# Sample pages for the NSA compression: both head groups in one load, turned by products with the identity

## The chip, the cores and the metric

The kernel runs on one core of a Trainium2 chip. The metric is the device time of one execution in microseconds. Every kernel is executed several times, and the median of the runs is given. The engines are named as in the profile: PE (TensorE, matrix products; PEld is its weight load), DVE (VectorE), ACT (ScalarE), POOL (GpSimd) and SP (SyncE, which here only issues transfers; SPq is its queue).

## The reference, cut to what matters

One inference step of a hybrid decoder layer: a prompt of 1024 positions and 8 samples with one new position and 512 cached positions each. The cache is paged, 128 positions to a page, 4 pages to a sample. Four head groups share the mixing: attention with a forget bias ("fox"), NSA (compressed, selected and window branch), pooling, and memory. The change touches the compression of the NSA group. For keys (kind 0) and values (kind 1) it takes the rows of each block of 64 positions and of each of the 2 head groups as one vector of 4096 numbers, adds a position term, and sends it through a small network:

```python
def nsa_compress(rows, pe, w1, w2):
    B, L, G, dh = rows.shape
    nb = L // NSA_BLOCK
    blk = rows.reshape(B, nb, NSA_BLOCK, G, dh) + pe[:, None, :].astype(rows.dtype)
    flat = jnp.transpose(blk, (0, 1, 3, 2, 4)).reshape(B, nb, G, NSA_BLOCK * dh)
    hid = jax.nn.silu(jnp.einsum('bngf,fe->bnge', flat, w1))
    return jnp.einsum('bnge,ed->bngd', hid, w2)
```

For the samples, `rows` are the pages of `cache_nsa_kv[page, position, kind, group, channel]`, with 4 kinds, 2 groups and 64 channels, so that the two groups of one kind and position lie side by side: 128 numbers, 512 bytes.

## The kernel before, in words

All five engines run one hand-written list of steps, `STEPS`, each in its own program. PE's part of a step runs in that order, and the other engines take its results in the same order. The steps that matter here:

- `project(m)` computes column tile m of the input projection for all 1032 positions: 72 products of 344 columns (three for each of 8 depths and 3 column chunks, L485 to L487), about 11.3 us at full clock. Its weights are loaded by SP (`load_w`, issue at L1879) and split into a high and a low part by POOL (L1778 and L1780).
- `natural(m)` turns a projected tile back to positions by rows, and copies it out through two banks, one copied by ACT ("A") and one by DVE ("D").
- `forget` computes running sums of the forget gates on DVE; SP then moves them (L1944), and only behind that does it issue weight tile 10.
- `pair` 0 to 7 (keys) and 8 to 15 (values) each bring the 4 pages of one sample into the layout of the compression: PE turns them into one bank (`pair_job`, L643), and ACT (even pairs) or DVE (odd pairs, L1483) copies the bank, 128 x 512, to FT. An even pair uses bank A and an odd one bank D; a job waits until the bank's last result has been copied.
- `compress(kind)` multiplies FT by the first weight matrix, which SP loads in four pieces of 1 MB (L1907) into two slots; a slot is loaded again when PE has read it. PE's products are at L661: 16 for each piece, shown as 32 records.
- `attend(0)`, `(1)`, `(2)` are the attention over the prompt: memory, fox, and selected with window.

SP issues all loads in one list. A quarter q is half a sample's pages of one kind, that is two pages: `load_pair(q)`. Quarters 0 to 3 are issued before weight tile 9, then 4 to 6, 7 to 9, 10 to 12 and 13 to 15 behind weight tiles 10, 11, 12 and 13, 16 to 19 before the fox attention, 20 to 22 with the first two compression weight pieces, 23 and 24 between the third and the fourth piece, 25 to 27 behind the fourth, and 28 to 31 when pairs 8 and 9 have been turned. A page's number is read from the page table (L1883) and then its transfers are issued (L1900): one for each head group, 64 partitions of two runs of 256 bytes. A partition j of a page's half holds positions 2j and 2j + 1 of the page (r = 0, 1).

PE turns a quarter's page pair with the transpose instruction, once for each group: the result has (r, channel) on its 128 partitions and (page, j) on its columns.

Order of PE's steps in the first stretch: project 8, forget, pair 0, project 9, pairs 1 and 2, project 10, natural 9, project 11, pair 3, natural 10, pair 4, project 12, natural 11, pair 5, natural 12, pairs 6 and 7, attend 1. In the second: project 13 and 14, natural 13, compress 0, project 15, pairs 8 to 11, project 16, natural 15, pairs 12 to 15, compress 1.

Of the kernel before, what the change touches and what calls it, by code (L numbers as in the profile page):

```python
# [29 lines left out]
P = 128  # L30
# [7 lines left out]
DH = 64  # L38
# [114 lines left out]
def build(nc, x_p, x_s, c_fox, c_lf, c_nsa, st_win, st_pool, c_mem, ptab, mem_p, norm_g, w_in, b_f, pe_, w1,  # L153
# [3 lines left out]
    with ExitStack() as ctx:  # L157
        def sb(name, shape, dt=F32):
            return ctx.enter_context(nc.sbuf_tensor(name, shape, dt))

        def sem(name):
            return ctx.enter_context(nc.semaphore(name))
# [16 lines left out]
        ident = sb("ident", [P, P])  # L179
# [75 lines left out]
        def pair_slot(q):  # L255


            if q < 16:
                where = PP[:, q * 256:(q + 1) * 256]
            elif 20 <= q < 28:  # L260
                where = NAT[:, (q - 20) * 512 + 256:(q - 19) * 512]
            else:
                where = VW[:, q % 4 * 256:(q % 4 + 1) * 256]
            return where.rearrange("p (a c) -> p a c", a=2)

        w1s = PP[:, :].rearrange("p (s j e) -> p s j e", s=2, j=8)
        HS = KW[:, 0:2 * R_ALL].rearrange("p (a r) -> p a r", a=2)
# [92 lines left out]
        s_pair = [sem(f"s_pair{n}") for n in range(NB)]  # L360
# [84 lines left out]
        def _(pe):  # L445
            mm, tr = nc.tensor.matmul, nc.tensor.transpose
            nA, nD = [0], [0]

            def job_a():

                if nA[0]:
                    pe.wait_ge(s_fA, nA[0])
                nA[0] += 1
                return bk(6)

            def job_d():

                if nD[0]:
                    pe.wait_ge(s_fD, nD[0])
                nD[0] += 1  # L460
                return bk(7)
# [174 lines left out]
            def pair_job(n, kind):  # L636

                out = job_a() if n % 2 == 0 else job_d()
                pe.wait_ge(s_pair[n], 128 * (kind + 1))
                for a in range(2):  # L640
                    q = 16 * kind + 2 * n + a
                    for g in range(2):
                        last = tr(out[:, (2 * g + a) * P:(2 * g + a + 1) * P],  # L643
                                  pair_slot(q)[:, g, :], ident[:, :])
                last.then_inc(s_TA if n % 2 == 0 else s_TD, 1)
                mark["pair", kind, n] = (s_TA, nA[0]) if n % 2 == 0 else (s_TD, nD[0])

# [268 lines left out]
            for step, n in STEPS:  # L916
# [10 lines left out]
                elif step == "natural":  # L927
                    if n == 18:
                        pe.wait_ge(s_fD, mark["cmp_scores", 0][1])
                    natural(n)  # L930
                elif step == "pair":
                    pair_job(n % 8, n // 8)
                elif step == "attend":
                    if n == 0:
# [920 lines left out]
        def _(sp):  # L1855
# [25 lines left out]
            def page(i):  # L1881

                return sp.value_load(ptb[0:1, bass.ds(i, 1)], min_val=0, max_val=c_fox.shape[1] - 1)  # L1883

            def load_pair(q):

                kind, n, half = q // 16, (q % 16) // 2, q % 2
                if q == 0:
                    sp.wait_ge(s_on, PHASE[0][1])
                if q == 20:  # L1890
                    sp.wait_ge(s_nst, 32)
                if q >= 28:
                    sem_, val = mark["pair", 1, (q - 28) // 2]
                    sp.wait_ge(sem_, val)
                for a in range(2):
                    pg = page(NPG * n + 2 * half + a)
                    for g in range(2):
                        src = c_nsa[0, bass.ds(pg, 1), :, kind, g, :].rearrange("o (j r) d -> (o j) r d", r=2)
                        dst = pair_slot(q)[a * DH:(a + 1) * DH, g, :].rearrange("p (r d) -> p r d", r=2)
                        sp.dma_start(dst, src).then_inc(s_pair[n], 16)  # L1900

            def load_w1(n):
                kind, c = n // 4, n % 4
# [31 lines left out]
            for q in range(4):  # L1935
                load_pair(q)
# [9 lines left out]
            for n in range(5):  # L1946
                load_w(10 + n)
                if n < 4:
                    for q in range(4 + 3 * n, 7 + 3 * n):
                        load_pair(q)  # L1950
# [4 lines left out]
            for q in range(16, 20):  # L1955
                load_pair(q)
# [36 lines left out]
            for g, w in enumerate(POOLW):  # L1993
                src = st_pool[0, :, 16 - w:15, g * DH:(g + 1) * DH]
# [62 lines left out]
            for m in (28, 29, 30):  # L2057
                load_w(m)
                n = m - 28
# [106 lines left out]
```

## Time and profile before

| | |
|---|---|
| median of 3 runs | 949.19 us (948.94 to 949.86) |
| profiled execution | 949.2 us, span 947.5 us |
| PE busy | 826.5 us (87%), 5755 products |
| DVE / ACT / POOL busy | 385.0 / 268.7 / 164.0 us |
| DMA | 79.45 MB in 110409 packets, 27237 of them under 512 B |
| granted clock of PE, mean | 0.946 of full speed |

The span is the time from the first to the last instruction of the profiled execution; 1.7 us of its time lie around it. Busy time is not the same as time that matters: an engine that waits for another costs nothing unless it is on the chain that ended last. That chain is the view to begin with. A line such as `L643` is a line of the kernel's source; `out<-in` gives the program's names of what is written and read. The bracket at the end of a timeline's row gives the idle time of the engine before it, and what ended it. The clock is given as a share: 1.00 is 2.4 GHz, 0.50 is 1.2 GHz.

### The profile page before, as it was taken

To read this page: it belongs to the slowest core of one execution; us is meant where nothing else is said; L and a number is where in the kernel's file an instruction comes from. 1 tells how busy PE (TensorE), PEld (TensorE's weight loads), DVE (VectorE), ACT (ScalarE), POOL (GpSimd) and SP (SyncE) were. 2 spreads that over 40 slices of the span, in tenths; PEclk is the share of its full clock that TensorE was granted. 3 is DMA by queue.
4 is the path that set the end of the run, shared out by engine and by line. 5 is a ranking of instruction groups with operands and counts; after the bars stand their busy time and mean duration, and the time that the engine had idled before them with its cause. 6 is when DMAs were issued, how large, how long until landed. Compare 5 with 4: busy or idle time off the path is not lost.

```text
span 947.5 us, 15437 instructions
## 1 busy us (share of the span) xinstructions
PE 826.5 (87%) x5755; PEld 680.9 (72%) x5755; DVE 385.0 (41%) x752; ACT 268.7 (28%) x624; POOL 164.0 (17%) x115
## 2 busy tenths in 40 slices
PE   3788997896999879895987999989999999699997
PEld 3788687893566878795964666659888878567775
DVE  3721734113664201201335767773823115434433
ACT  4612710112544202200124444540113225221211
POOL 4645001331000301046211000001431110000000
PEclk9979998996999989997899999989999999879999
DMA  7410002235411234131031000001124547256531
GB/s 231 160 48 23 1 21 50 55 75 171 150 45 49 81 106 128 24 105 45 1 114 42 2 1 2 1 4 47 46 82 143 149 135 201 84 188 193 180 121 48
DMA packets 110409, 79.45 MB, mean 84 GB/s; under 512 B 27237, under 2 KB 104308, under 8 KB 110264
## 3 DMA queue, kind: packets, MB, share of 16 engines
q1 hardware_dynamic: 108880, 77.66, 27.4%
q10 hardware_dynamic: 1456, 0.82, 0.4%
q8 instruction: 46, 0.75, 0.3%
q14 instruction: 27, 0.22, 0.1%
HBM read 68.81 MB, written 13.85 MB: 87 GB/s over the span
## 4 chain that ended last, share of the span: by engine, by line
PE 71%; DVE 9%; SPq 5%; issue 4%; DMA 4%; POOL 3%; ACT 3%; DVEq 0%; POOLq 0%; ACTq 0%
PE PS L485 14%; PE PS L487 13%; PE PS L486 13%; PE PS L567 6%; PE PS L613 5%; PE PS L592 4%; PE PS L661 3%; SPq L1900 2%; PE PS L577 2%; PE PS L871 2%; DVE AUG L1390 1%; PE PS L787 1%; PE PS L617 1%; DVE stat L1340 1%; SPq L2022 1%
## 5 line engine op out<-in xcount | busy, mean ns | idle before, releaser
L485 PE MATMUL PS<-HH,WH 128*128 128x344 f32 (+2 forms) x824 | 285.9, 347 | 21.7 <-POOL WL L1780 13.8
L486 PE MATMUL PS<-HL,WH 128*128 128x344 f32 (+2 forms) x824 | 280.5, 340 | 0.0
L487 PE MATMUL PS<-HH,WL 128*128 128x344 f32 (+2 forms) x824 | 280.0, 340 | 0.0
L485 PEld LDWEIGHTS PS<-HH,WH 128*128 128x128 f32 x824 | 162.0, 197 | 35.1 <-POOL WL L1780 14.4
L486 PEld LDWEIGHTS PS<-HL,WH 128*128 128x128 f32 x824 | 161.7, 196 | 6.4
L487 PEld LDWEIGHTS PS<-HH,WL 128*128 128x128 f32 x824 | 161.4, 196 | 6.8
L1778 POOL TENSOR_TENSOR WH<-WR,onesc 128x1024 fp32r<-128x1024 f32 x31 | 60.4, 1949 | 560.8 <-issue 224.9
L1105 ACT ACTIVATE PP<-PS,stat 128x640 f32<-128x640 f32 (+7 forms) x96 | 67.8, 710 | 106.9 <-DVE stat L1340 106.9
L1340 DVE TENSOR_REDUCE stat<-PS 128x1 f32<-128x640 f32 (+7 forms) x96 | 65.1, 720 | 65.1 <-PE PS L580 64.7
L1780 POOL TENSOR_TENSOR WL<-WR,WH 128x1024 fp32r<-128x1024 f32 x31 | 79.0, 2548 | 2.4
L592 PE MATMUL PS<-ident,PP 128*128 128x128 f32 x472 | 66.3, 277 | 10.7 <-DVE AUG L1390 8.2
L567 PE MATMUL PS<-AUG 64*128 64x512 f32 (+3 forms) x288 | 61.8, 536 | 9.8 <-ACT PP L1105 7.4
L592 PEld LDWEIGHTS PS<-ident,PP 128*128 128x128 f32 x472 | 53.7, 141 | 16.6 <-DVE AUG L1390 14.0
L1390 DVE COPY AUG<-PS 128x512 f32<-128x512 f32 (+3 forms) x80 | 48.9, 627 | 8.3 <-PE PS L592 7.7
L613 PE MATMUL PS<-AUG,NAT 128*64 128x128 f32 (+1 forms) x640 | 47.4, 290 | 4.0 <-ACT AUG L997 1.9
L661 PE MATMUL PS<-OB,PP 128*128 128x161 f32 x256 | 41.5, 328 | 9.7 <-DMA PP<-in_nsa_w 5.2
L1311 DVE COPY VS<-PS 64x8 f32<-64x8 f32 x8 | 1.4, 170 | 118.2 <-PE PS L487 118.2
L661 PEld LDWEIGHTS PS<-OB,PP 128*128 128x128 f32 x256 | 40.2, 211 | 10.8 <-DMA PP<-in_nsa_w 6.0
L567 PEld LDWEIGHTS PS<-AUG 64*128 64x128 f32 x288 | 25.2, 195 | 30.4 <-issue 19.3
L613 PEld LDWEIGHTS PS<-AUG,NAT 128*64 128x64 f32 x640 | 35.5, 137 | 11.4 <-DVE AUG L1390 4.1
L997 ACT ACTIVATE AUG<-PS 128x128 f32<-128x128 f32 (+5 forms) x88 | 40.9, 465 | 7.5 <-PE PS L592 7.0
L1638 DVE COPY NAT<-PS 128x512 f32<-128x512 f32 x16 | 11.1, 692 | 62.9 <-PE PS L787 62.7
(318 smaller groups left out, 862.9 us busy)
## 6 DMA issues: line engine op xcount, KB each, us to landing
WR<-in_w_in SPq DMA_DIRECT2D x26, 512.0 KB, 4.3
PP<-in_nsa_w SPq DMA_DIRECT2D x8, 1024.0 KB, 6.1
OB<-in_x_prompt SPq DMA_DIRECT2D x8, 512.0 KB, 5.8
out<-NAT SPq DMA_DIRECT2D x2, 2048.0 KB, 7.7
PP<-in_cache_fox_kv SPq DMA_DIRECT2D x32, 128.0 KB, 2.3
PP<-in_cache_nsa_kv SPq DMA_DIRECT2D x64, 64.0 KB, 1.9
PP<-in_state_nsa_win SPq DMA_DIRECT2D x16, 256.0 KB, 3.0
PP<-in_cache_mem_kv SPq DMA_DIRECT2D x16, 256.0 KB, 3.3
```

The source lines that it names most:

```text
L485: mm(out, lhs[0], rhs[0], start=(k == 0), stop=False)
L486: mm(out, lhs[0], rhs[1], start=False, stop=False)
L487: return mm(out, lhs[1], rhs[0], start=False, stop=(k == KC - 1))
L567: mm(bk(score_bank(u, e) + c // 4)[:, 0:n * P], q[r, i * P:(i + 1) * P], k[r, (k0 + c) * P:(k0 + c + n) * P], start=True, stop=False)
L592: last = tr(bk(4 + g % 3)[:, (b - c) * P:(b - c + 1) * P], PP[:, p0:p0 + P], ident[:, :])
L613: mm(bk(7)[e * DH:(e + 1) * DH, 0:wide * P], v, p_, start=(b == 0), stop=(b == (1 if what == "mem" else nk - 1)))
L661: last = mm(bk(e)[:, 0:R_ALL + 1], w1s[:, n % 2, jj, e * P:(e + 1) * P], FT[:, j, :], start=(j == 0), stop=(j == NJ - 1))
L1105: last = act1(PP[:, c:c + nk * P], flat(score_bank(u, e), nk), ACT.Exp, bias=stat[:, k:k + 1], accum_out=stat[:, 16 + k:17 + k])
L1340: v.tensor_reduce(stat[:, k:k + 1], flat(score_bank(u, e), nk), AX.X, ALU.max, negate=True).then_inc(s_nm, 1)
L1390: v.tensor_copy(turned_p(u - 1, e, c, n), bk(4 + g % 3)[:, 0:n * P]).then_inc(s_cD, 1)
L1778: g.tensor_tensor(hi_, WR[:, s, :, :], ones, ALU.mult).then_inc(s_wcp, 1)
L1780: g.tensor_tensor(lo_, WR[:, s, :, :], hi_.bitcast(F32), ALU.subtract).then_inc(s_split, 1)
```

## The change

A page's keys or values of one kind come in one transfer with both head groups (two runs of 512 bytes for each of 64 partitions) instead of two transfers (two runs of 256 bytes each). 64 transfers are issued instead of 128, and the semaphore counts are halved to match. In the buffer, a partition now holds (r, group, channel) where it held (group, r, channel). The turn of one group therefore reads 64 columns for r = 0 and 64 for r = 1, which are no longer adjacent: each is a plain product with the identity as the moving operand, which writes 64 partitions of the bank. A pair job has 8 products where it had 4 transpose instructions. Bank, copies and everything after them are unchanged.

```diff
-            return where.rearrange("p (a c) -> p a c", a=2)
+            return where.rearrange("p (r c) -> p r c", r=2)
...
-                pe.wait_ge(s_pair[n], 128 * (kind + 1))
+                pe.wait_ge(s_pair[n], 64 * (kind + 1))
                 for a in range(2):
                     q = 16 * kind + 2 * n + a
                     for g in range(2):
-                        last = tr(out[:, (2 * g + a) * P:(2 * g + a + 1) * P],
-                                  pair_slot(q)[:, g, :], ident[:, :])
+                        for r in range(2):
+                            last = mm(out[r * DH:(r + 1) * DH, (2 * g + a) * P:(2 * g + a + 1) * P],
+                                      pair_slot(q)[:, r, g * DH:(g + 1) * DH], ident[:, :], start=True, stop=True)
...
                     pg = page(NPG * n + 2 * half + a)
-                    for g in range(2):
-                        src = c_nsa[0, bass.ds(pg, 1), :, kind, g, :].rearrange("o (j r) d -> (o j) r d", r=2)
-                        dst = pair_slot(q)[a * DH:(a + 1) * DH, g, :].rearrange("p (r d) -> p r d", r=2)
-                        sp.dma_start(dst, src).then_inc(s_pair[n], 16)
+                    src = c_nsa[0, bass.ds(pg, 1), :, kind, :, :].rearrange("o (j r) g d -> (o j) r (g d)", r=2)
+                    sp.dma_start(pair_slot(q)[a * DH:(a + 1) * DH], src).then_inc(s_pair[n], 16)
```

## Rows read from the trace of the kernel before

**Rows 1.** Page, section 4: shares of the ending chain by line.
```profile
PE PS L485 14%; PE PS L487 13%; PE PS L486 13%; PE PS L567 6%; PE PS L613 5%; PE PS L592 4%; PE PS L661 3%; SPq L1900 2%; PE PS L577 2%; PE PS L871 2%; DVE AUG L1390 1%; PE PS L787 1%; PE PS L617 1%; DVE stat L1340 1%; SPq L2022 1%
```

**Rows 2.** Lines L1900 and L2022: issue in ns, min/median/max, first and last start.
```profile
L1900 SPq DMA_DIRECT2D PP<-in_cache_nsa_kv x64: 537/537/1108, 125.3 to 214.1; - x64
...
L2022 SPq DMA_DIRECT2D PP<-in_cache_nsa_kv x64: 332/333/1544, 696.8 to 907.4; - x64
```

**Rows 3.** Chain of waits in two stretches: start us, us, what.
```profile
170.80 2.01 DMA PP<-in_cache_nsa_kv
...
343.17 0.55 SPq L1900
343.90 0.54 SPq L1900
```

**Rows 4.** Chain: four turns, eight turns, eight products (16 records).
```profile
201.82 0.44 PE PS L643 x4
...
219.52 1.91 PE PS L643 x8
...
284.69 1.02 PE PS L613 x16
```

**Rows 5.** Timeline of SP's queue: start us, us, line, what.
```profile
125.30 16.64 SPq L1900 DMA_DIRECT2D PP<-in_cache_nsa_kv  x16
...
143.19 0.40 SPq L1879 DMA_DIRECT2D WR<-in_w_in  x1
...
162.45 0.42 SPq L1879 DMA_DIRECT2D WR<-in_w_in  x1
163.86 11.50 SPq L1900 DMA_DIRECT2D PP<-in_cache_nsa_kv  x12
...
348.56 0.59 SPq L1907 DMA_DIRECT2D PP<-in_nsa_w  x1
```

**Rows 6.** Timeline of POOL, splits of tiles 9 and 10 [idle before].
```profile
149.88 1.89 POOL L1778 TENSOR_TENSOR WH<-WR,onesc 128x1024 fp32r<-128x1024 f32 x1 [54.82 <-DMA WR<-in_w_in]
...
169.21 2.35 POOL L1780 TENSOR_TENSOR WL<-WR,WH 128x1024 fp32r<-128x1024 f32 x1
```

**Rows 7.** Timeline of PE, projection 9 and pair 2 [idle before].
```profile
154.25 0.65 PE L485 MATMUL PS<-HH,WH 128*128 128x344 f32 x1 [2.55 <-POOL WL L1780]
...
172.94 0.78 PE L643 MATMUL PS<-ident,PP 128*128 128x128 f32 x4 [4.24 <-DMA PP<-in_cache_nsa_kv]
```

**Rows 8.** Stretches: PE, PEld, DVE, ACT, POOL busy; granted clock; DMA.
```profile
154.30:159.50 5.20, 5.20 (x18) 5.20 (x19) 4.91 (x6) 0.00 (x0) 0.00 (x0) 0.50 0.00 0
173.50:176.50 3.00, 3.00 (x13) 3.00 (x12) 0.00 (x0) 1.11 (x1) 0.00 (x0) 0.50 0.17 38
219.30:221.50 2.20, 2.12 (x10) 1.38 (x8) 0.74 (x2) 1.09 (x1) 2.12 (x2) 0.50 0.11 42
388.00:391.60 3.60, 2.45 (x16) 1.65 (x16) 1.58 (x2) 2.18 (x3) 0.00 (x0) 1.00 0.12 27
```

**Rows 9.** Timeline of PE, compression pieces and pairs 8 to 15.
```profile
346.29 6.32 PE L661 MATMUL PS<-OB,PP 128*128 128x161 f32 x32 [2.16 <-DMA PP<-in_nsa_w]
354.36 4.66 PE L661 MATMUL PS<-OB,PP 128*128 128x161 f32 x32 [1.75 <-DMA PP<-in_nsa_w]
...
372.03 1.09 PE L643 MATMUL PS<-ident,VW 128*128 128x128 f32 x8 [1.06 <-ACT KCs L997]
...
387.98 1.23 PE L643 MATMUL PS<-ident,NAT 128*128 128x128 f32 x8 [0.79 <-ACT NAT L997]
...
391.02 0.63 PE L643 MATMUL PS<-ident,VW 128*128 128x128 f32 x4 [0.55 <-DMA VW<-in_cache_nsa_kv]
```

**Rows 10.** Timeline of DVE, copy of pair 15.
```profile
391.68 1.07 DVE L1483 COPY OB<-PS 128x512 f32<-128x512 f32 x1 [1.35 <-PE PS L643]
```

**Rows 11.** Timeline of PE, first scores of two attention phases.
```profile
222.88 3.78 PE L567 MATMUL PS<-AUG 64*128 64x512 f32 x8 [1.47 <-DVE OB L1483]
...
494.21 1.99 PE L567 MATMUL PS<-AUG 64*128 64x512 f32 x8 [0.98 <-DVE VW L1328]
```

## The prediction

> **What bounds the kernel now.** I read the page's chain first, then the chain piece by piece, then the queue of SP, POOL and PE over the two stretches in which sample pages are turned (124 to 223 us and 303 to 394 us). The chain is TensorE for the most part: the three products of every projection are 40% of it, and the issuing of the page loads (SP at L1900) holds 2% [rows 1]. That 2% is what the change can take away, and TensorE is where it pays. A load is issued in 537 ns [rows 2] and lands 2.0 us later; two successive issues of one page start 0.73 us apart [rows 3], so each load that goes takes 0.73 us out of SP's queue. There are 128 loads, 4 per quarter q; 64 go.
>
> Where does SP's queue end a wait? Three places. (a) Project 9: weight tile 9 is issued at 143.19, behind the first 16 page loads (125.30 to 141.94) [rows 5]; POOL splits it from 149.88 [rows 6], and PE, done with pair 0 at 154.25 - 2.55 = 151.7, waits 2.55 us for POOL before project 9 [rows 7]. (b) Project 10: pair 2, which stands before it on PE, waits 4.24 us for pages [rows 7] that are issued only after weight tile 10 at 162.45 [rows 5]. (c) Compression of the keys: its fourth weight piece is issued at 348.56 behind eight page loads [rows 5], and PE waits 1.75 us for it [rows 9]. Elsewhere the pages are ahead of PE, save 0.55 us before pair 15 [rows 9].
>
> **What the change removes: SP's issues.** Per quarter it takes 2 of 4 loads, 1.46 us. I keep 537 ns and 2.0 us for the new load, which has as many pieces, each twice as long. The bounds for its issue are 0.33 us, what L2022 takes for a page of 64 KB, and 1.1 us, the longest at L1900 [rows 2]. The lower one would bring no more than 0.4 us, since in (a) to (c) something else is late next.
>
> (a) The first four quarters end 8 x 0.73 = 5.8 us earlier, so tile 9 is issued at 137.4 and split by about 148.4 (154.2 - 5.8). Then pair 0 is late next, and project 9 starts straight behind it, at about 152.2. Today it runs at half clock to 159.5 [rows 8]; without the gap I expect full clock. What project 9 gains so is idle time again: tile 10 cannot leave before 162.45, because its issue waits for the forget sums, which the change does not touch, and POOL ends its split at 169.21 + 2.35 = 171.56 [rows 6].
> (b) Pair 2 needs four pages after 163.86. Three issues fewer stand before the last (one for each page before it, and the last page has a single load): 170.80 [rows 3] - 4 x 0.73 = 167.9, landed at 169.9 instead of 172.8. With its 1 to 2 us (below) it ends at 170.9 to 171.9, and the split ends at 171.56: project 10 starts at about 171.8 instead of 173.72. That is **-1.9 us**, its new cost on pair 2 included. Project 10 runs its first 3 us at half clock today [rows 8]; as pair 2 stands in part of that stretch, I take another **-0.5** (0 to -1.3).
> (c) The fourth piece leaves 4 x 0.73 = 2.9 us earlier, at 345.6, and lands at 351.4. Late next is PE's own third piece, which ends at 346.29 + 6.32 = 352.6. So the fourth starts 1.8 us earlier, not 2.9: **-1.8 us**. The third piece's weight load shares the DMA engines with half as many page packets; I give that nothing (0 to -0.4).
> The 16 loads of the last four quarters get 5.8 us shorter too, but win only the 0.55 us before pair 15, which the next part swallows. Loads at 227 and 305 us run beside attention and projections 13 and 14; cover is many us, so they are worth nothing. The waits on pair semaphores (64 instead of 128 counts for half the loads) stay where they are.
>
> **What it adds: TensorE.** A pair job is now 4 turns of 128 x 128: 0.44 us at full clock, 1.91/2 = 0.96 us at half [rows 4]. It becomes 8 products with 64 columns of pages held and 128 columns of identity moving, in plain f32. That form is in the trace: the weighing of values at L613 (held 128 x 64, moving 128 x 128, two halves of the output in turn) takes 1.02 us for 8 products, shown as 16 records [rows 4]. That is 0.58 more than 0.44; a part of it is the start of the first one, which today's job has too, so I take **1.0 us, +0.5 for each job**, and at half clock 2.0, +1.0. The rest of a job, one copy of 128 x 512 (1.07 us, [rows 10]), keeps its shape. Which of the 16 jobs lie on the path?
> Pairs 0, 1: hidden in the idle time of (a). Pair 2: counted in (b). Pair 3: hidden by VectorE, which first takes project 11. Pair 4 stands directly before project 12: +0.5. Pair 5 is at full clock, its copy gates the rest of natural 12: +0.5. Pairs 6 and 7 run back to back at half clock, 1.91 us [rows 4, 8], before attention: +2.0. Together **+3.0**.
> Pairs 8 and 9 stand back to back (372.03, 1.09 us), then 10 and 11 wait for their copies [rows 9]; the second of each couple follows VectorE's copy of the one before. The series 8, 9, copy, 11 grows by 3 x 0.5: +1.5 on the start of project 16. After natural 15 the series is 12, 13, copy, 15: pair 13 starts behind pair 12 and a copy of natural 15 that end together, so 0.4 to 0.5 of pair 12's growth shows, 13 and 15 add 1.0, and the 0.55 us wait for pages before pair 15 [rows 9] is gone: +0.9. Together **+2.4**.
>
> **Sum**: -1.9 - 0.5 - 1.8 + 3.0 + 2.4 = +1.2 us. The profiled execution took 949.2 us (span 947.5), the median of the runs is 949.19, so no correction between them: **950.4 us**. Own range 948.0 to 951.8. This kernel's measurement can tell about 0.2%, 1.9 us, from no change.
>
> **Rivals.**
> *The clock comes back earlier.* The change puts plain products where turns were. At 219.3 to 221.5 PE is busy 2.12 of 2.20 us with turns alone, and the clock stays at its lower level of 1.2 GHz [rows 8]; the first unit of the forgetting attention then starts at that level and takes 3.78 us for its scores, where the like unit of the later attention, at 2.4 GHz, takes 1.99 [rows 11]. If the products hold or raise the clock there, pairs 6 and 7 cost 2.0 instead of 4.0 us and the first scores gain 1.8: 950.4 - 2.0 - 1.8 = **946.6 us**. For it: those rows. Against it: from 388.0 to 391.6 us PE does nothing but turns, with gaps, and the clock stays full [rows 8], so turns do seem to hold it. The Trainium skill (TensorE: Matmul & The Clock Gate, Part 4: PE-mode transpose) says that turns don't count as busy for the clock in the way of products; by that rule this rival would be the likeliest. The trace agrees at 220 us and disagrees at 388 to 391.6 us. Chance 0.22.
> *The clock falls at pairs 12 to 15* (ends slower). They stand between gaps of 0.55 to 0.79 us today, at full clock [rows 8, 9]. If the level there is the lower one, jobs 12, 13 and 15 take 2.0 instead of 1.0 us: 950.4 + 3.0 = **953.4 us**. It decides if the level falls before pair 13, near 390 us; later it costs under 1 us. For it: the same pattern of turns, copies and gaps between 214 us and pair 6 does lose the clock, by 219.3 [rows 8]. Chance 0.18.
> *The halves don't run side by side.* Then a job takes 8 x 0.24 = 1.9 us, +0.96 more for each of some 11 growths on the path (6 counted up to attention, with the two at half clock double and pair 2; 5 after): +11, **961 us**. Against it stands L613's 1.02 us; for it, that all eight products here move the same identity. Chance 0.07.
> *The loads don't get cheaper*: twice the bytes cost SP twice, 1.1 us. Then (a), (b) and (c) fall, pair 2 adds 0.5, and 949.2 + 3.0 + 2.4 + 0.5 = **955.1 us**. Against it: weight loads of 512 KB are issued in 0.4 to 0.6 us (0.42 at 162.45) [rows 5]. Chance 0.05.
>
> **How the numbers follow.** Forecast 0.48, rivals 0.22, 0.18, 0.07 and 0.05. The range goes from just below the first rival to the second, 946.2 to 953.5: the last two rivals (0.12) and tails (0.08) are outside. Faster by over 0.2% (below 947.3): the first rival and a rest of the forecast, less the first rival's upper part: 0.24. Slower (over 951.1): second to fourth rivals less a part of the second, and the forecast's upper end: 0.30. Within 0.2%: 0.46.
>
> **What would show it.** SP: page periods 0.73 us shorter, tile 9 issued near 137.4, the fourth compression piece near 345.6. PE: project 9 right behind pair 0 at full clock; project 10 near 171.8; the fourth piece directly behind the third, no wait for weights. A pair job of 16 records in 1.0 us at full clock. First scores of the forgetting attention at 223.5 (222.88 - 1.9 - 0.5 + 3.0), and [rows 9] pair 15 behind pair 13's copy. The forecast is wrong if the granted clock differs from today's in 214 to 231 or in 386 to 399 us, or if a job's length isn't 1.0 us.

## The result, and the profile after

The changed kernel took 945.21 us (median of 9 runs, 942.46 to 946.32), the kernel before, run between them, 949.86 (9 runs, 947.97 to 953.75). The ratio is 0.994, with a 95% interval of 0.9921 to 0.996: faster by 0.6%. The forecast was 950.4 in a range of 946.2 to 953.5, so it had the sign wrong and the time fell 1 us below the range. The profiled execution took 943.73 us, its span 942.0 (before 949.2 and 947.5).

Page of the changed kernel: span, and the chain's shares by engine and by line. Its line numbers are one higher than before's in the body, and one lower from L1899 (the page loads, L1900 before) on.
```profile
span 942.0 us, 15629 instructions
...
PE 74%; DVE 9%; issue 4%; POOL 4%; DMA 3%; ACT 3%; SPq 2%; DVEq 0%; POOLq 0%; ACTq 0%
PE PS L485 15%; PE PS L487 14%; PE PS L486 14%; PE PS L567 6%; PE PS L613 5%; PE PS L592 4%; PE PS L662 3%; PE PS L788 2%; PE PS L872 2%; PE PS L577 2%; DVE AUG L1391 1%; DVE stat L1341 1%; PE PS L617 1%; DMA PP<-in_nsa_w 1%; POOL OB L1843 1%
```
The page loads, 2% of the chain before [rows 1], are no longer among the lines that it names. The chain itself, in order of time, still runs over them, ahead of pair 2 and of the fourth compression piece (start us, us, what):
```profile
165.70 0.54 SPq L1899
166.99 2.31 DMA PP<-in_cache_nsa_kv
169.44 1.09 PE PS L644 x16
...
339.65 0.54 SPq L1899
340.23 6.74 DMA PP<-in_nsa_w
```

SP's queue: the lines view of L1899 (issue in ns, min/median/max), then its timeline (start us, us).
```profile
L1899 SPq DMA_DIRECT2D PP<-in_cache_nsa_kv x32: 537/537/719, 125.3 to 195.3; - x32
```
```profile
125.32 9.82 SPq L1899 DMA_DIRECT2D PP<-in_cache_nsa_kv  x8
...
136.79 0.84 SPq L1880 DMA_DIRECT2D WR<-in_w_in  x1
158.47 2.98 SPq L1943 DMA_DIRECT2D KW<-AUG  x4
161.50 0.42 SPq L1880 DMA_DIRECT2D WR<-in_w_in  x1
162.93 7.19 SPq L1899 DMA_DIRECT2D PP<-in_cache_nsa_kv  x6
...
340.23 0.59 SPq L1906 DMA_DIRECT2D PP<-in_nsa_w  x1
```
A load of twice the bytes is issued in the same 537 ns as before [rows 2], and half of them go. Four quarters take 9.8 us, not 16.6 [rows 5], so here each issue that goes saves 0.85 us. Weight tile 9 leaves at 136.8 and the fourth compression piece at 340.2. Tile 10 leaves at 161.5, 0.95 us earlier than before, though the forecast had nothing move it.

TensorE's timeline (start us, us, [idle before]); L644 is a pair job, 16 records each.
```profile
147.78 0.60 PE L707 MATMUL PS<-ident,lf 128*4 128x128 f32 x4
...
151.63 1.98 PE L644 MATMUL PS<-ident,PP 128*64 128x128 f32 x16
153.54 0.61 PE L485 MATMUL PS<-HH,WH 128*128 128x344 f32 x1
...
169.44 1.09 PE L644 MATMUL PS<-ident,PP 128*64 128x128 f32 x16 [3.08 <-DMA PP<-in_cache_nsa_kv]
...
181.90 0.27 PE L536 MATMUL PS<-ident,AUG 128*128 128x128 f32 x1
...
215.81 1.97 PE L644 MATMUL PS<-ident,PP 128*64 128x128 f32 x32
219.15 1.99 PE L567 MATMUL PS<-AUG 64*128 64x512 f32 x8 [1.36 <-DVE OB L1484]
```
```profile
340.26 4.65 PE L662 MATMUL PS<-OB,PP 128*128 128x161 f32 x32 [1.78 <-DMA PP<-in_nsa_w]
347.01 4.66 PE L662 MATMUL PS<-OB,PP 128*128 128x161 f32 x32 [2.10 <-DMA PP<-in_nsa_w]
...
364.68 1.97 PE L644 MATMUL PS<-ident,VW 128*64 128x128 f32 x32 [1.06 <-ACT KCs L998]
...
384.43 1.97 PE L644 MATMUL PS<-ident,VW 128*64 128x128 f32 x32 [0.32 <-ACT OB L998]
```
Two pair jobs take 1.97 us, at 215.81 as at 364.68. At 215.81 that is what two jobs of turns took before at half clock (1.91, [rows 4]), because here the clock is full. The first scores take 1.99 instead of 3.78 us [rows 11].

Windows of the changed kernel (columns as [rows 8]).
```profile
154.30:159.50 5.20, 5.20 (x35) 5.20 (x34) 4.01 (x5) 0.49 (x1) 0.00 (x0) 1.00 0.01 3
170.60:173.60 3.00, 3.00 (x20) 3.00 (x21) 0.00 (x0) 1.11 (x1) 0.00 (x0) 1.00 0.76 207
213.00:218.00 5.00, 4.19 (x56) 3.37 (x56) 1.94 (x3) 1.64 (x2) 1.46 (x1) 1.00 0.08 29
```
The third number from the right is the granted clock. All three of these stretches, the starts of projections 9 and 10 and the jobs before attention, run at the upper level, 2.4 GHz, where before they ran at 1.2 GHz [rows 8].

**Stages.** I cut each trace at rows of TensorE: t0, the first turn of the forget sums (147.78 above); n9 and n11, the first instruction of natural jobs 9 and 11 (181.90 and 209.80); att, the first scores of the forgetting attention (219.15); 3rd, the scores of its third unit; p13, projection 13; c1 and c2, the first instructions of the two compressions (327.59 and 388.97); p8, pair 8 (364.68). Two traces of a kernel stand as a/b; the experiments are told below.

| us | before | after | loads only | products only | tile 9 first | turns in 5-7 | after, new order | before, new order | hybrid |
|---|---|---|---|---|---|---|---|---|---|
| start to t0 | 147.8/145.7 | 147.8/148.8 | 149.7/149.6 | 147.3/147.3 | 145.7 | 149.4/145.3 | 147.8 | 145.6 | 147.7 |
| t0 to n9 | 38.6/38.5 | 34.1/33.8 | 34.8/34.7 | 39.4/39.1 | 38.6 | 35.2/36.0 | 29.3 | 27.3 | 30.8 |
| n9 to n11 | 27.1/27.1 | 27.9/27.9 | 27.2/27.2 | 27.9/27.9 | 27.1 | 27.9/27.9 | 27.9 | 32.9 | 27.9 |
| n11 to att | 9.5/9.4 | 9.4/9.3 | 9.4/9.4 | 10.3/9.4 | 9.3 | 8.4/9.3 | 9.4 | 9.0 | 9.4 |
| att to 3rd | 17.0/15.9 | 14.8/15.1 | 16.9/16.9 | 14.8/14.8 | 14.6 | 15.9/15.3 | 14.8 | 15.9 | 14.8 |
| 3rd to p13 | 63.2/64.9 | 63.2/64.3 | 63.2/63.2 | 63.2/63.2 | 63.2 | 64.3/63.2 | 63.2 | 64.4 | 63.2 |
| p13 to c1 | 30.4/30.4 | 30.5/30.2 | 30.4/30.4 | 28.9/28.9 | 30.4 | 30.2/28.9 | 30.5 | 30.2 | 30.4 |
| c1 to p8 | 38.6/39.0 | 37.1/36.6 | 36.3/36.4 | 41.7/41.8 | 39.0 | 36.1/37.9 | 35.0 | 36.4 | 34.3 |
| p8 to c2 | 22.2/23.4 | 24.3/24.3 | 22.0/22.0 | 24.3/24.3 | 23.4 | 24.3/24.3 | 24.3 | 23.0 | 22.4 |
| c2 to end | 553.3/551.9 | 553.0/553.3 | 552.6/552.8 | 553.9/553.8 | 551.8 | 553.8/551.2 | 552.2 | 554.3 | 554.1 |

The first row varies by 4 us between traces of one kernel (149.4 and 145.3), so nothing in it counts as an effect. Other rows vary too: "after" and "turns in 5-7" have the same code up to pair 5, and from t0 to n9 they took 34.1, 33.8, 35.2 and 36.0 us. A difference below about 1 us in a single trace, and below about 2 us in that row, is not an effect yet. By the means of two traces each, the change gained 4.5 us from t0 to n9, 1.5 from att to 3rd and 2.0 from c1 to p8; it lost 0.8 from n9 to n11 and 1.5 from p8 to c2. With the two traces of "turns in 5-7" the gain from t0 to n9 is 3.7.

### The profile page after: what moved, and what is told of

It is laid out like the page before. It is cut to its first block, busy times and chain, and to the rows that moved or that the text cites. A ratio compares the mean times of both kernels' runs of the same rounds, so it can differ in the third digit from the quotient of the medians.

```text
span 942.0 us, 15629 instructions
## 1 busy us (share of the span) xinstructions
PE 828.0 (88%) x5947; PEld 683.2 (73%) x5947; DVE 384.4 (41%) x752; ACT 269.1 (29%) x624; POOL 164.0 (17%) x115
## 3 DMA queue, kind: packets, MB, share of 16 engines
q1 hardware_dynamic: 99664, 77.65, 27.2%
## 4 chain that ended last, share of the span: by engine, by line
PE 74%; DVE 9%; issue 4%; POOL 4%; DMA 3%; ACT 3%; SPq 2%; DVEq 0%; POOLq 0%; ACTq 0%
PE PS L485 15%; PE PS L487 14%; PE PS L486 14%; PE PS L567 6%; PE PS L613 5%; PE PS L592 4%; PE PS L662 3%; PE PS L788 2%; PE PS L872 2%; PE PS L577 2%; DVE AUG L1391 1%; DVE stat L1341 1%; PE PS L617 1%; DMA PP<-in_nsa_w 1%; POOL OB L1843 1%
## 5 line engine op out<-in xcount | busy, mean ns | idle before, releaser
L1779 POOL TENSOR_TENSOR WH<-WR,onesc 128x1024 fp32r<-128x1024 f32 x31 | 61.3, 1976 | 551.9 <-issue 222.6
L592 PEld LDWEIGHTS PS<-ident,PP 128*128 128x128 f32 x472 | 53.6, 141 | 16.6 <-DVE AUG L1391 14.0
L1750 DVE TENSOR_TENSOR PP<-PS,WR 128x1024 f32<-128x1024 f32 (+1 forms) x9 | 11.0, 1223 | 62.1 <-PE PS L487 42.1
```

What stands on the lines that cost most here:

```text
L592: last = tr(bk(4 + g % 3)[:, (b - c) * P:(b - c + 1) * P], PP[:, p0:p0 + P], ident[:, :])
L1779: g.tensor_tensor(hi_, WR[:, s, :, :], ones, ALU.mult).then_inc(s_wcp, 1)
```

## The experiments

Three questions were open. Is the gain the loads' or the products'? Was it tile 9 or the pages that held the first stretch? And did products hold the clock before attention?

**The changed kernel again**, no edit.

> The changed kernel again, beside the kernel before on the same chip, as the measure for the runs of this call. Both theories expect 4 to 6 us less than before (ratio 0.994 to 0.996), tile 9 split by about 147, project 10 at about 170.5 and the first scores of the fox attention in 2.0 us.

Measured: 944.53 us (6 runs) beside 950.30 of the kernel before (25 runs), ratio 0.9928 (0.9901 to 0.9955). The next three experiments have the same comparison. The gain repeats, and the trace is the second one of "after" in the table.

**Loads alone.** The changed kernel's loads, with turns; an operand then is a page's row half of both head groups, so the turned pages land in other places and the compressions work on exchanged rows. Every instruction keeps its shape.
```diff
-                    for g in range(2):
-                        for r in range(2):
-                            last = mm(out[r * DH:(r + 1) * DH, (2 * g + a) * P:(2 * g + a + 1) * P],
-                                      pair_slot(q)[:, r, g * DH:(g + 1) * DH], ident[:, :], start=True, stop=True)
+                    for r in range(2):
+                        last = tr(out[:, (2 * r + a) * P:(2 * r + a + 1) * P],
+                                  pair_slot(q)[:, r, :], ident[:, :])
```

> The loads of the change with the turns of before: one transfer for each page, and four transpose instructions over the 128 adjacent columns for each job. The turned groups and rows come out in swapped places, so the compression of the samples computes on exchanged data; the work is the same in kind and number. Theory Q (all gain comes from SP's shorter queue; the products only cost, 0.5 us for each job on the path, some 5 of them before and after attention): about 942.5 against 949.5 of before, 2 to 3 us below the changed kernel, and the fox attention's first scores at full clock, 2.0 us. Theory P (plain products in the place of transposes keep the clock up before the attention): pairs 6 and 7 at half clock, first scores 3.8 us, no faster than the changed kernel, 945 to 947.

Measured: 943.97 us (8 runs), ratio 0.9935 (0.9904 to 0.9965). TensorE's timeline, then a window:
```profile
170.97 1.09 PE L643 MATMUL PS<-ident,PP 128*128 128x128 f32 x4 [5.59 <-DMA PP<-in_cache_nsa_kv]
...
217.49 2.11 PE L643 MATMUL PS<-ident,PP 128*128 128x128 f32 x8
220.96 3.78 PE L567 MATMUL PS<-AUG 64*128 64x512 f32 x8 [1.35 <-DVE OB L1483]
```
```profile
172.00:175.00 3.00, 3.00 (x13) 3.00 (x12) 0.00 (x0) 1.11 (x1) 0.00 (x0) 0.56 0.73 197
```
The time lies between the two theories, and each is half right: the gain is there without the products, as theory Q says, and the clock is at half at pairs 6 and 7 and in the first scores (3.78 us), as theory P says.

**Products alone.** The kernel before, with its four loads per quarter.
```diff
-                        last = tr(out[:, (2 * g + a) * P:(2 * g + a + 1) * P],
-                                  pair_slot(q)[:, g, :], ident[:, :])
+                        for r in range(2):
+                            last = mm(out[r * DH:(r + 1) * DH, (2 * g + a) * P:(2 * g + a + 1) * P],
+                                      pair_slot(q)[:, g, r * DH:(r + 1) * DH], ident[:, :], start=True, stop=True)
```

> The products of the change with the loads of before: two transfers for each page in the old layout, eight products with the identity for each job. Theory Q: project 9 still waits for POOL until about 154.2, pair 2 for pages until 172.9, the clock is lost before pairs 6 and 7, and each job on the path costs more: +3 to +6 us over before, about 954. Theory P: pairs 6 and 7 and the first scores of the fox attention run at full clock: -2 to +1 us, about 949.

Measured: 951.86 us (12 runs), ratio 1.0008 (0.9989 to 1.0028): no difference that shows, and between the 949 and 954 of the two theories. TensorE's timeline, the fourth compression piece:
```profile
354.15 6.32 PE L662 MATMUL PS<-OB,PP 128*128 128x161 f32 x32 [4.28 <-DMA PP<-in_nsa_w]
```
c1 comes 1.5 us earlier here, but the piece's load does not, so PE waits 4.28 us for it and then works at half clock: c1 to p8 is 3.0 us longer. One more trace of each half followed, at 944.12 us for the loads and 952.17 for the products, beside 947.97 of the kernel before.

> The loads of the change with turns in all jobs once more (turned groups and rows come out in swapped places). Theory P: half clock at pairs 6 and 7 and 9.3 to 9.5 us from natural 11 to the first scores. Theory R: full clock in about half of such looks, 8.4 us. The end of project 8 to natural 11 should be 61.9 us again.

> The products of the change with the loads of before once more. Theory P: pairs 6 and 7 at full clock, 2.0 us, natural 11 to first scores 9.3 to 10.3 us. Theory R: half clock in about half of such looks, then pairs 6 and 7 take 3.8 to 4.0 us and that length is 11 us or more. The end of project 8 to natural 11 should be 67.3 us again.

So the gain is the loads', and the products come out near zero over the whole kernel. The table shows why. Beside "loads only", the changed kernel pays 0.8 us from n9 to n11 (pair 4), 0.5 from c1 to p8 and 2.3 from p8 to c2. It gets back 1.9 from att to 3rd, where its clock is full and that of "loads only" half, and 0.8 from t0 to n9, where the clock at the start of projection 10 differs (0.56 in the window above, against 1.00 in [170.60:173.60] of after). The 0.8 can't be put down to the products, since the same code varies by 2.2 us there. The sum is +0.9 us, and the medians differ by 0.6, which their intervals don't separate.

**Tile 9 ahead of the pages**, in the kernel before. This gives tile 9 its early issue without taking a single page issue away.
```diff
+            load_w(9)
...
-            load_w(9)
```
The added line stands right behind `load_w(8)`, ahead of quarters 0 to 3; the removed one stood behind them.

> The kernel before with one move in SP's list: the load of weight tile 9 is issued ahead of the first 16 page loads instead of behind them. Both theories: POOL has split tile 9 before 148, VectorE's first pass over the forget sums (4 x 1024) takes 0.7 us instead of 2.07 because POOL no longer works beside it, tile 10 leaves SP 1 to 1.4 us earlier, and project 9 starts behind pair 0. Theory Q: pair 2 still waits for its pages, until about 171.8, so project 10 gains 1 us only: 948 to 948.5. If the collision of POOL and VectorE is not the cause of the 2.07 us, that pass stays at 2.07 and project 10 stays at 173.7: no change.

Measured: 950.51 us (12 runs), ratio 1.000 (0.9979 to 1.0022). Timelines of VectorE and TensorE, and a window:
```profile
151.07 0.68 DVE L1526 TENSOR_SCALAR OB<-OB 4x1024 f32<-4x1024 f32 x1
```
```profile
169.97 1.09 PE L643 MATMUL PS<-ident,PP 128*128 128x128 f32 x4 [7.11 <-DMA PP<-in_cache_nsa_kv]
```
```profile
171.00:174.00 3.00, 3.00 (x12) 3.00 (x11) 0.00 (x0) 1.10 (x1) 0.00 (x0) 0.50 0.22 49
```
Projection 9 is early, and most of that becomes idle time before pair 2: 7.11 us instead of 4.24 [rows 7]. VectorE's pass takes 0.68 us, as expected, so tile 10 and the pages behind it leave earlier. Counted from t0, pair 2 starts 0.9 us earlier than in the kernel before (24.2 us behind t0 instead of 25.2 and 25.1) and projection 10 0.6 us earlier, but projection 10 then stays longer at half clock, and t0 to n9 stays 38.6. The 948 to 948.5 us that were expected did not come; the interval, 2 us to each side, could hide a gain of that size. The early tile alone does not bring the gain of the change. The trace is that of the fastest of the 12 executions (944.76 us).

**Turns in the three jobs before attention.** The changed kernel with turns in pairs 5, 6 and 7 of the keys; with the new loads their rows come out exchanged.
```diff
+                        if kind == 0 and n >= 5:
+                            last = tr(out[:, (2 * g + a) * P:(2 * g + a + 1) * P],
+                                      pair_slot(q)[:, g, :], ident[:, :])
+                            continue
                         for r in range(2):
```

> The changed kernel with pairs 5, 6 and 7 turned by transpose instructions as before (over the 128 adjacent columns, so that for these three samples' keys groups and rows come out exchanged; the work is the same in kind as before). All that stands ahead of pair 5 is the changed kernel's. Theory P (plain products keep the clock up in this stretch, turns don't): the clock falls before pairs 6 and 7, they take 1.9 to 2.1 us although their work is half, and the fox attention starts no earlier than in the changed kernel (natural 11 to first scores 9.3 to 9.4 us). Theory R (the clock at this place depends on when the stretch falls in the run, not on the kind of instruction): full clock as in the changed kernel, pairs 6 and 7 in 0.9 us, natural 11 to first scores about 8.0 us, and 1.4 us less in all, about 943.

Measured: 945.25 us (9 runs), ratio 0.9945 (0.9922 to 0.9968). TensorE's timeline:
```profile
218.02 0.60 PE L644 MATMUL PS<-ident,PP 128*128 128x128 f32 x4
218.96 0.66 PE L644 MATMUL PS<-ident,PP 128*128 128x128 f32 x4 [0.35 <-DVE NAT L1333]
220.97 1.99 PE L567 MATMUL PS<-AUG 64*128 64x512 f32 x8 [1.35 <-DVE OB L1488]
```
Turns stand before attention, and the clock is full all the same: a job takes 0.6 us and the first scores 1.99. From natural 11 to the first scores it is 8.4 us, 0.9 less than in the changed kernel. The 943 us of theory R did not come: the whole is no faster than the changed kernel. The kernel before took 950.99 us (14 runs) in this comparison, which holds for the experiments below too. A second trace of it was taken, and one of the kernel before beside it.

> The changed kernel with turns for pairs 5 to 7 once more (for these the turned data come out exchanged). Theory P: half clock at pairs 6 and 7 this time, 1.9 to 2.1 us, natural 11 to first scores 9.3 to 9.5 us. Theory R: full clock again or not, as chance has it; with full clock 8.4 us.

> The kernel before once more, for one more look at its clock. Theory P (products keep the clock before the fox attention, turns mostly lose it): half clock at pairs 6 and 7, 1.9 to 2.1 us. Theory R (chance of the moment, independent of the kind of instruction): full clock in about half of such looks, 0.9 us. The length from the end of project 8 to natural 11 should be 65.7 us again, since it is set by waits.

Measured: 941.07 us for the turns in pairs 5 to 7 and 947.92 for the kernel before (beside 947.97 of the same kernel). The kernel before had half clock at pairs 6 and 7 again, though its first scores took 1.99 us this time. Windows of the second trace with turns in pairs 5 to 7:
```profile
214.60:215.60 1.00, 0.96 (x5) 0.97 (x6) 0.00 (x0) 0.36 (x1) 0.00 (x0) 0.50 0.00 0
215.60:218.00 2.40, 1.36 (x9) 0.88 (x7) 1.46 (x2) 1.64 (x2) 0.00 (x0) 0.95 0.22 84
```
Here the clock was at half from about 212.3 to 215.8 us, and then came back while TensorE did nothing but turns. The count over all traces: with turns in every job the clock was half at pairs 6 and 7 in six of six (before twice, "loads only" twice, tile 9 first, before in the new order in part); with products in every job it was full in six of six (one fell to half at 218.4 and was back by 221.7); with products up to pair 4 and turns behind, full in two of two (in the second from 0.3 us into pair 6 on). Counted by whether the clock fell at all between natural 11 and the first scores, it is six of six with turns in every job, one of six with products, one of two with both. How long it stayed down varies within a kernel: the two traces of the kernel before took 3.78 and 1.99 us for the first scores. The natural jobs in between are turns in every kernel. So the kind of the three jobs right before attention does not decide it. Whether the products of pairs 0 to 4 do, or the moment at which this stretch is reached, stays open.

**A new order of issues.** If the number and place of SP's issues are what binds, order should bring more than the change. Tile 9 goes ahead of all pages; tile 10 and quarters 4 to 9 go ahead of the wait for the forget sums; the last compression piece (`load_w1(3)`) goes straight behind the third. First on the changed kernel:
```diff
+            load_w(9)
...
-            load_w(9)
+            load_w(10)
+            for q in range(4, 10):
+                load_pair(q)
...
-            for n in range(5):
-                load_w(10 + n)
-                if n < 4:
-                    for q in range(4 + 3 * n, 7 + 3 * n):
-                        load_pair(q)
+            load_w(11)
+            for q in range(10, 13):
+                load_pair(q)
+            load_w(12)
+            for q in range(13, 16):
+                load_pair(q)
+            load_w(13)
+            load_w(14)
...
+            load_w1(3)
...
-            load_w1(3)
```

> The changed kernel with SP's list put in another order: weight tiles 9 and 10 and the pages of quarters 4 to 9 are issued before SP waits for the forget sums, quarters 10 to 15 behind tiles 11 and 12, and the compression's fourth weight piece ahead of quarters 23 and 24. Expected: no wait of PE for pages before pair 2, project 10 starts at about 17.5 + 2.1 = 19.6 us behind the end of project 8 instead of 22.7, fourth piece behind the third without a wait: -3 and -2 us, about 940 against 944.5 of the changed kernel. If PE's projections are held by POOL's splits instead, -2 us only.

Measured: 938.26 us (5 runs), ratio 0.9871 (0.9843 to 0.9899). TensorE's timeline:
```profile
163.77 1.97 PE L644 MATMUL PS<-ident,PP 128*64 128x128 f32 x32
...
340.06 4.65 PE L662 MATMUL PS<-OB,PP 128*128 128x161 f32 x32 [0.25 <-DMA PP<-in_nsa_w]
```
That is 1.7 us better than expected. Pairs 1 and 2 run back to back without a wait for pages, and the fourth compression piece waits 0.25 us instead of 2.10. The same edit on the kernel before:

> The kernel before with the same new order of SP's list. It tells whether the cheaper loads matter once the pages don't stand in the way of weights. Theory Q (the change pays through SP's queue alone): this order gives the kernel before more than the change did, -6 us or more to 943, and the changed kernel with this order is then no better than this one, or worse by what its products cost (up to 2 to 3 us). If the loads must be fewer in any order: tile 11 comes late behind the pages (24 loads take until about 167), project 11 waits, and this kernel stays at 947 or above.

Measured: 940.89 us (5 runs), ratio 0.9899 (0.987 to 0.9927). Timelines of SP and TensorE:
```profile
142.43 23.83 SPq L1900 DMA_DIRECT2D PP<-in_cache_nsa_kv  x24
...
169.38 0.42 SPq L1879 DMA_DIRECT2D WR<-in_w_in  x1
```
```profile
177.90 0.42 PE L485 MATMUL PS<-HH,WH 128*128 128x344 f32 x1 [3.96 <-POOL WL L1780]
```
The order alone brings about 10 us, twice what the change brought. Both expectations were half right: it gains more than the change did, and tile 11 is late. Six quarters are 24 issues and 23.8 us here, so tile 11 leaves at 169.4, eight us later than in the reordered changed kernel (161.1), and projection 11 waits 3.96 us for its split: n9 to n11 grows to 32.9. That is where fewer issues still pay under the better order. The change adds 2.6 us by the medians, but the ranges (934.20 to 938.87, 937.57 to 942.32) overlap; the stages from t0 to n11 give it 3.0 in one trace of each.

**A hybrid.** The reordered changed kernel, with the values (pairs 8 to 15) loaded by two transfers per page and turned by turns as before. There issues are hidden and TensorE is not.
```diff
-                pe.wait_ge(s_pair[n], 64 * (kind + 1))
+                pe.wait_ge(s_pair[n], (64, 192)[kind])
...
+                        if kind:
+                            last = tr(out[:, (2 * g + a) * P:(2 * g + a + 1) * P],
+                                      pair_slot(q)[:, g, :], ident[:, :])
+                            continue
...
+                    if kind:
+                        for g in range(2):
+                            src = c_nsa[0, bass.ds(pg, 1), :, kind, g, :].rearrange("o (j r) d -> (o j) r d", r=2)
+                            dst = pair_slot(q)[a * DH:(a + 1) * DH, g, :].rearrange("p (r d) -> p r d", r=2)
+                            sp.dma_start(dst, src).then_inc(s_pair[n], 16)
+                        continue
```

> The reordered changed kernel with the values (pairs 8 to 15) loaded and turned as before, two transfers for each page and transpose instructions, and the keys (pairs 0 to 7) as in the change. The products of pairs 8 to 15 cost 2.1 us on the path (24.3 against 22.2 us from pair 8 to the second compression), and the doubled loads there were worth 0.55 us: so 1.5 to 2 us less than the reordered changed kernel, about 938.5. If the clock falls at pairs 12 to 15 with turns, no gain.

Measured: 935.96 us (4 runs, 934.13 to 936.82), ratio 0.9849 (0.9821 to 0.9877): the lowest median of all, 1.5% below the kernel before. TensorE's timeline:
```profile
376.20 0.66 PE L644 MATMUL PS<-ident,VW 128*128 128x128 f32 x4 [0.60 <-ACT OB L1002]
377.61 0.63 PE L644 MATMUL PS<-ident,VW 128*128 128x128 f32 x4 [0.75 <-DMA VW<-in_cache_nsa_kv]
```
p8 to c2 falls from 24.3 to 22.4 us, though 0.75 us of waiting for pages is back before pair 15. The median is 2.3 us below that of the reordered changed kernel, but their ranges overlap, and the two profiled spans are 934.9 (hybrid) and 934.2. The hybrid's trace gains 1.9 us in this stage and loses 1.5 from t0 to n9 and 1.9 behind c2, where the two kernels run the same code. So the stage shows the gain, and the whole time does not yet.

## Why the prediction was wrong

It forecast +1.2 us; by the means of two traces the spans differ by -4.0 (942.85 against 946.85), by the medians -4.7. The miss is 5.2 us. Three terms make 7.1 of it: 2.1 from t0 to n9, 4.1 from n11 to 3rd, 0.9 from p8 to c2. The rest, +1.9, is for the most part in stretches that the change doesn't touch (+1.6 before t0, +0.6 behind c2), and so is the scatter between traces.

**What was right.** The mechanism on SP: 537 ns for the new load, 0.68 to 0.85 us for each issue that goes where I took 0.73, tile 9 at 136.8 (137.4 forecast). Project 9 ran at full clock, if 1.3 us later than forecast (153.54), since pair 0 itself was at half clock (1.98 us); as forecast, nothing hangs on that. (c): the fourth compression piece was to gain 1.8 us and c1 to p8 fell by 2.0 (1.5 between the first two traces). That the size fits is luck in part. Late next was the landing, not the third piece as I wrote, since that ran at full clock (4.65 us, not 6.32 [rows 9]); the piece landed 6.7 us after its issue, where I had counted 5.8, and the wait, which I had expected to vanish, grew from 1.75 to 2.10. A job of products takes 1.09 us alone and two take 1.97, against 0.60 for a job of turns: +0.5, as I took. Pair 4's +0.5 was measured as +0.8. From p8 to c2 I forecast +2.4: it is +2.3 between "loads only" and the changed kernel, +1.9 between the two reordered kernels that differ there, and +1.5 against the kernel before by its two traces. One of those, at 23.4, had its clock lowered at pair 11 (two jobs in 1.53 us, not 1.10). The rivals "halves don't run side by side" and "the loads don't get cheaper" are refuted by 1.97 us for two jobs and by 537 ns. (The 11 growths of the first leave one out: pair 2, pairs 4 and 5, and pairs 6 and 7 doubled are 7, and 5 come behind attention. That makes 962 us, not 961.) "The clock falls at pairs 12 to 15" is refuted too: those jobs took 1.97 us for two in every trace with products.

**Step (b), the first stretch: forecast -2.4, measured -4.5 (-3.7 with the two traces that share the code up to pair 5).** The failed part is the bound behind pair 2, that tile 10's split ends at 171.56 because "its issue waits for the forget sums, which the change does not touch". The change does touch them. Timelines of the kernel before, VectorE and POOL:
```profile
152.67 2.07 DVE L1526 TENSOR_SCALAR OB<-OB 4x1024 f32<-4x1024 f32 x1
```
```profile
151.85 2.34 POOL L1780 TENSOR_TENSOR WL<-WR,WH 128x1024 fp32r<-128x1024 f32 x1
```
And of the changed kernel:
```profile
153.12 0.68 DVE L1527 TENSOR_SCALAR OB<-OB 4x1024 f32<-4x1024 f32 x1
```
```profile
142.55 1.89 POOL L1779 TENSOR_TENSOR WH<-WR,onesc 128x1024 fp32r<-128x1024 f32 x1 [47.46 <-DMA WR<-in_w_in]
...
167.54 2.34 POOL L1781 TENSOR_TENSOR WL<-WR,WH 128x1024 fp32r<-128x1024 f32 x1
```
Before, VectorE's pass over the forget sums ran beside POOL's second split pass of tile 9 and took 2.07 us. With tile 9 early, POOL is long done and the pass takes 0.68. The forget sums, the transfers behind them, tile 10 and the pages behind it come 0.95 us earlier. The pass stood on the chain of the kernel before, so it could be read beforehand that its length counts (start us, us, what):
```profile
152.67 2.08 DVE OB L1526
```
The split then ends at 169.88 (167.54 + 2.34), 1.7 us before my bound, and no longer holds anything: pair 2 ends last, and projection 10 starts right behind it, near 170.5 where I had 171.8. That pair 2 began at 169.44 (169.9 forecast) hides two errors that partly cancel: its pages left SP 0.9 us earlier than I took, and the last landed in 2.31 us, not 2.0. The other 0.7 us of the split is tile 10's own loading: from issue to the first split pass 4.07 us against 4.79. It is 5.1 in the second trace of the kernel before and 3.9 to 4.2 in every other trace with this order, three of them with the old page loads, so I have no cause for it.

The second failed part is projection 10's clock: I took -0.5 for its half-clock start, with -1.3 as the bound, and it ran at full clock from its start in both traces of the changed kernel. That is not a sure property of the change. Projection 10's first 3 us in the two traces with turns in pairs 5 to 7, whose code is the changed kernel's up to there (one row from each):
```profile
172.25:175.25 3.00, 3.00 (x15) 3.00 (x14) 0.00 (x0) 1.11 (x1) 0.00 (x0) 0.64 0.77 217
168.54:171.54 3.00, 3.00 (x12) 3.00 (x11) 0.00 (x0) 1.11 (x1) 0.00 (x0) 0.51 0.84 210
```
From projection 10's start to n9 it is 11.4 us in both traces of the changed kernel, 12.4 and 12.8 in these two, and 12.9 in both of the kernel before. So part of the measured gain is a state of the clock that comes and goes, and what decides it stays open. "Loads only" (0.56) lies within the same spread. "Tile 9 first" shows that the end of the collision is not enough by itself: there the pages are still late, and what it brings is lost to the clock.

**Pairs 5 to 7: forecast +2.5, measured -0.1; and att to 3rd, forecast 0, measured -1.5.** This is the rival "the clock comes back earlier", at 946.6 us and a chance of 0.22. The failed step is the half clock that I took for pairs 6 and 7 and left standing for the first scores. Both traces of after show the full clock: 1.97 us for two jobs and 1.99 for the first scores. The rival's price (2.0 + 1.8) was about right: 4.1 by the two stages. In these is pair 5's +0.5, of which 0.1 shows (pair 6 starts 6.0 us behind n11, not 5.9), since natural 12 behind pair 5 was at half clock before. The gain from att to 3rd is the less certain part: "tile 9 first", with the old loads and turns, has 14.6 us there too. Taken with the extra 2.1 of (b) the rival gives 950.4 - 3.8 - 2.1 = 944.5, close to the two medians (945.2 and 944.5), but only because the misses left over nearly cancel. I had asked whether the products hold the clock in their own place, and for that the runs give no proof: turns in the same place, behind products, left it full as well. The Trainium skill's rule (TensorE: Matmul & The Clock Gate, Part 4: PE-mode transpose), that turns don't count as busy for the clock in the way of products, fits the six traces with turns in every job. By it alone the two traces with turns in pairs 5 to 7 should have had half clock at pairs 6 and 7, and these took 0.60 to 0.76 us each, where 0.96 is the price at half clock [rows 4].

**The range.** It ended just below the first rival, as if that rival had no companion. Two terms that were each given a most likely value could both come out on the good side: the clock of projection 10 and the rival. The runs don't show that they have one cause, since with turns in pairs 5 to 7 the first was at its lower level and the second at the upper; but nothing kept them from coming together. The two should have been added: 946.6 less the 0.8 us left of that term's bound is 945.8. That is still 0.6 above the median; the rest is the issue of tile 10 and of the pages behind it, which I had treated as fixed.

## What to carry over

On a queue that issues small transfers one by one, count issues and ask what stands behind them; here halving their number gained 0.6%, and moving the urgent ones ahead gained 1.0% without touching the transfers. Pay for fewer issues with TensorE time only where a wait for the transfers ends last: here for the keys, but not for the values. When a load becomes earlier, look at what the engine that takes it up was colliding with, not only at who waits for it. And where the granted clock changes in a stage, take several traces of the same code before you credit the change with it.

## What the runs showed of the hardware

A pass of VectorE over 4 x 1024 f32 values in SBUF (L1526) takes 0.68 us alone. When it starts beside POOL's 128 x 1024 subtraction, it does not end before that one. Timelines of the second trace of "products only", VectorE and POOL:
```profile
152.20 1.57 DVE L1527 TENSOR_SCALAR OB<-OB 4x1024 f32<-4x1024 f32 x1
```
```profile
150.87 2.36 POOL L1781 TENSOR_TENSOR WL<-WR,WH 128x1024 fp32r<-128x1024 f32 x1
```
It ended 0.54 us behind POOL (153.77 and 153.23). In all four traces with such an overlap it ended 0.54 to 0.55 us behind POOL, having taken 1.57 to 2.15 us; where POOL was done before it started it took 0.68 us in all ten. Not every instruction of VectorE is held up: the scan right before it (L1521) took 1.27 us beside POOL in the kernel before, and 1.27 without POOL in the changed one. It looks as if the pass needed something that POOL holds until its instruction ends; the traces don't say what.

One 64-row transfer of 512-byte runs costs its queue 537 ns, as one of 256-byte runs does, and landed 2.4 us after its issue in the median (2.2 at least), against 2.1 (2.0 at least) for the load of before. Single executions of one kernel on one chip lie up to 10 us apart (943.81 to 954.12 over 25 runs of the kernel before), and in the traces much of that is there before t0 and where the granted clock drops. From t0 to n9 four traces of the same code differ by 2.2 us. A difference of that size in a stage needs more than one trace of each kernel before it is an effect.
